# A fused decoder layer whose first projection takes its activations already turned

## The reference

```
def rmsnorm(x, g):
    xf = x.astype(jnp.float32)
    y = xf * lax.rsqrt(jnp.mean(xf * xf, axis=-1, keepdims=True) + EPS)
    return (y * g.astype(jnp.float32)).astype(x.dtype)

def mixer_sublayer(x, k_buf, v_buf, pool_buf, pos0, w_in, w_out, w_pool, pool_scale, sinks, g_pre, g_post):
    h = rmsnorm(x, g_pre)
    proj = jnp.einsum('ntd,de->nte', h, w_in)
    ...                       # q, k, v -> sliding-window attention; u -> causal pooling
    out = jnp.einsum('nte,ed->ntd', jnp.concatenate([a, pl], axis=-1), w_out)
    return x + rmsnorm(out, g_post), new_k, new_v, new_pool

def ffn_sublayer(x, w_up, w_down, g_pre, g_post):
    h = rmsnorm(x, g_pre)
    a = jnp.square(jax.nn.relu(jnp.einsum('ntd,df->ntf', h, w_up)))
    return x + rmsnorm(jnp.einsum('ntf,fd->ntd', a, w_down), g_post)
```

## Time and profile before

| what | value |
|---|---|
| three runs | 2047.56, 2049.05, 2049.23 us, median 2049.05 |
| the profiled execution, its own time | 2047.78 us |
| its span, first to last instruction | 2046.0 us |
| PE busy | 1973.5 us, 96% |
| DVE, ACT, POOL busy | 62%, 60%, 44% |
| mean granted TensorE clock | 0.987 |

### The profile page before, as it was taken

The page is one execution under the profiler, slowest core; times in us unless marked ns, Lnnn a source line. Parts: engine busy times, 40 slices in busy tenths (PEclk is TensorE's granted clock), DMA queues, the critical chain, the costliest instruction groups (busy, mean ns, idle before and its releaser), DMA issues.

```text
span 2046.0 us, 39225 instructions
## 1 busy us (share of the span) xinstructions
PE 1973.5 (96%) x15450; PEld 1941.7 (95%) x15450; DVE 1272.8 (62%) x1966; ACT 1236.2 (60%) x1823; POOL 890.9 (44%) x619
## 2 busy tenths in 40 slices
PE   7999999999988899999999999989999999999998
PEld 6999999899978899999999999989999999999998
DVE  3455543622258776676676676666666666666687
ACT  5234421422264466776776777767777777777784
POOL 0000022211125666766666666654544454444472
PEclk9999998999989899999999999999999999999999
DMA  5411121252233356556556556795656556565542
GB/s 172 165 62 61 55 73 57 77 175 84 92 127 118 122 176 205 170 185 203 174 182 202 177 181 200 228 318 182 213 191 207 181 180 204 185 213 191 182 158 89
DMA packets 271342, 328.16 MB, mean 160 GB/s; under 512 B 8192, under 2 KB 236936, under 8 KB 270063
## 3 DMA queue, kind: packets, MB, share of 16 engines
q1 hardware_dynamic: 267680, 315.66, 47.4%
q10 hardware_dynamic: 3479, 9.99, 1.3%
HBM read 253.79 MB, written 74.22 MB: 160 GB/s over the span
## 4 chain that ended last, share of the span: by engine, by line
PE 59%; DVE 4%; issue 2%; DMA 1%; POOL 1%; ACT 0%; DVEq 0%; SPq 0%; POOLq 0%; ACTq 0%
PE banks L2248 20%; PE banks L2250 19%; PE banks L2249 19%; DVE mlp_rows L1689 3%; DVE quads L1671 1%; DMA mlp_kept<-mlp_rows 1%; DMA mlp_part<-mlp_kept 1%; PE banks L2266 0%; DVE x_tok L1813 0%; ACT mlp_hi L1182 0%; DVE splits L1645 0%; POOL mlp_rows L871 0%; POOL mlp_rows L873 0%; ACT mlp_rows L1176 0%; ACT splits L1159 0%
## 5 line engine op out<-in xcount | busy, mean ns | idle before, releaser
L2248 PE MATMUL banks<-mlp_part,splits 128*128 128x272 f32 x1792 | 517.8, 289 | 6.0 <-DVE y_sum L1668 2.5
L2250 PE MATMUL banks<-mlp_part,splits 128*128 128x272 f32 x1792 | 517.0, 288 | 0.0
L2249 PE MATMUL banks<-mlp_part,splits 128*128 128x272 f32 x1792 | 516.1, 288 | 0.0
L2248 PEld LDWEIGHTS banks<-mlp_part,splits 128*128 128x128 f32 x1792 | 336.6, 188 | 7.4 <-ACT splits L1159 7.0
L2249 PEld LDWEIGHTS banks<-mlp_part,splits 128*128 128x128 f32 x1792 | 340.8, 190 | 0.0
L2250 PEld LDWEIGHTS banks<-mlp_part,splits 128*128 128x128 f32 x1792 | 336.6, 188 | 0.0
L1671 DVE TENSOR_TENSOR y_sum<-y_sum,banks 128x272 f32<-128x272 f32 x416 | 182.2, 438 | 187.7 <-PE banks L2250 187.6
L2248 PE MATMUL banks<-s_part,splits 128*128 128x272 f32 x960 | 279.1, 291 | 7.8 <-ACT splits L1159 3.2
L2250 PE MATMUL banks<-s_part,splits 128*128 128x272 f32 x960 | 278.4, 290 | 0.0
L2249 PE MATMUL banks<-s_part,splits 128*128 128x272 f32 x960 | 277.2, 289 | 0.0
L1857 PE MATMUL banks<-acts_hi,w_hi 128*128 128x272 f32 x1184 | 253.1, 295 | 9.4 <-DVE uT L1357 4.1
(11 more groups left out here) (265 smaller groups left out, 4429.2 us busy)
## 6 DMA issues: line engine op xcount, KB each, us to landing
raw_down<-in_w_down SPq DMA_DIRECT2D x128, 512.0 KB, 4.4
raw_up<-in_w_up SPq DMA_DIRECT2D x120, 512.0 KB, 7.8
mlp_part<-mlp_kept SPq DMA_DIRECT2D x56, 1088.0 KB, 8.3
mlp_kept<-mlp_hi SPq DMA_DIRECT2D x32, 952.0 KB, 4.5
mlp_kept<-mlp_rows SPq DMA_DIRECT2D x32, 952.0 KB, 5.7
w_raw<-in_w_in SPq DMA_DIRECT2D x40, 512.0 KB, 3.5
w_raw<-in_w_out SPq DMA_DIRECT2D x32, 512.0 KB, 3.4
x_kept<-x1T SPq DMA_DIRECT2D x8, 544.0 KB, 2.8
```

Source lines behind the costliest of these rows:

```text
L2248: nc.tensor.matmul(out, wh, xh, start=first, stop=False, skip_group_check=not STARTS[i])
L2249: nc.tensor.matmul(out, wh, xl, start=False, stop=False, skip_group_check=not STARTS[i])
L2250: ins = nc.tensor.matmul(out, wl, xh, start=False, stop=j == pairs - 1, skip_group_check=not STARTS[i])
```

## The change

The host gives x a second time as x_cols, already turned: partition p holds, for each of the 16 tiles, the 544 tokens of feature 128 k + p. It also gives the five norm vectors as one block of columns, vec_cols.

- SP loads vec_cols straight into vecs and x_cols two tiles at a time into x_raw, 8 loads of 557 KB, interleaved with units 0 to 3. x_raw lies where acts_lo lies (tile by tile the same bytes), so the low part of a tile overwrites its raw x.
- No transposes of x, and none of the vectors.
- ACT makes the high part from SBUF, then squares the whole tile into one of two halves of sq_tmp. From the third tile on, the square waits until PE has summed the tile that used this half.
- DVE makes the low part in place, and waits for the high part and for the square.
- PE sums the squares of a tile over partitions with 5 matmuls of one column (`first_sums`, fp32, each two instructions on the engine), issued one tile late, into columns of bank 7. DVE adds the 16 columns per token with two reductions.
- `spread_scales(0)` moves from the end of unit 3 to the middle of unit 4, between its column blocks.
- START_SPLITS, after which tiles the units 1 to 3 are split, goes from 5, 7, 11 to 3, 7, 11.
- POOL's two waits for x and the squares ahead of its masks are gone, as is ACT's issue of four vector loads.

```diff
+        x_raw = at("x_raw", H_AT + KT * T * 4, [P, KT, T])
-        START_SPLITS = {0: 0, 5: 1, 7: 2, 11: 3}
+        START_SPLITS = {0: 0, 3: 1, 7: 2, 11: 3}
...
-            sp.dma_start(pre_rows[:], g_pre_mix[0].rearrange("(k p) -> k p", p=P)).then_inc(vec_landed[0], 16)
+            def load_x(i):
+                sp.dma_start(x_raw[:, 2 * i:2 * i + 2, :], x_cols[:, 2 * i:2 * i + 2, :]).then_inc(x_landed[i], 16)
+
+            sp.dma_start(vecs[:], vec_cols).then_inc(vec_landed[0], 16)
             load_x(0)
...
-                    if pair + kq == 0:
-                        load_x(1)
+                    if pair == 0:
+                        for i in ((1, 2), (3, 4), (5, 6), (7,))[kq]:
+                            load_x(i)
...
-            gp.wait_ge(x_turned, KT)
-            gp.wait_ge(squares, 2 * TOK)
...
             for kt in range(KT):
-                act.wait_ge(x_turned, kt + 1)
-                nc.scalar.activation(acts_hi[:, kt, :], flat(2 * x_slot(kt), T), ACT.Copy, scale=g_pre[:, kt:kt + 1]).then_inc(h_hi, 1)
+                act.wait_ge(x_landed[kt // 2], 16)
+                nc.scalar.activation(acts_hi[:, kt, :], x_raw[:, kt, :], ACT.Copy, scale=g_pre[:, kt:kt + 1]).then_inc(h_hi, 1)
+                if kt >= 2:
+                    act.wait_ge(x_summed, kt - 1)
+                nc.scalar.activation(sq_tmp[:, kt % 2 * T:(kt % 2 + 1) * T], x_raw[:, kt, :], ACT.Square).then_inc(squares, 1)
                 if kt in START_SPLITS:
                     split(START_SPLITS[kt])
-                n = kt - (KT - 2 * TOK)
-                if n >= 0:
-                    half, c = divmod(n, TOK)
-                    r = tok_rows[c]
-                    act.wait_ge(x_landed[half][c], 16)
-                    if n > 0:
-                        act.wait_ge(squares, n)
-                    nc.scalar.activation(uT[0:r].rearrange("p e n -> p (e n)")[:, 0:D // 2],
-                                         x_tok[0:r, c, half * (D // 2):(half + 1) * (D // 2)], ACT.Square,
-                                         accum_out=ss_half[0:r, half, c:c + 1]).then_inc(squares, 1)
             take_root(0)
             split(4)
...
-            dve.wait_ge(pre_ready, 1)
+            dve.wait_ge(vec_landed[0], 16)
             for kt in range(KT):
                 dve.wait_ge(h_hi, kt + 1)
-                nc.vector.scalar_tensor_tensor(out=acts_lo[:, kt, :], in0=flat(2 * x_slot(kt), T), scalar=g_pre[:, kt:kt + 1],
+                dve.wait_ge(squares, kt + 1)
+                nc.vector.scalar_tensor_tensor(out=acts_lo[:, kt, :], in0=x_raw[:, kt, :], scalar=g_pre[:, kt:kt + 1],
                                                in1=acts_hi[:, kt, :].bitcast(F32), op0=ALU.mult, op1=ALU.subtract).then_inc(h_lo, 1)
                 if kt in START_SPLITS:
                     split(START_SPLITS[kt])
-            dve.wait_ge(squares, 2 * TOK)
-            step(nc.vector.tensor_tensor(ss[:], ss_half[:, 0, :], ss_half[:, 1, :], ALU.add))
+            dve.wait_ge(consts, 3)
+            dve.wait_ge(x_summed, KT)
+            by_tile = banks[:, 7, P:P + TOK * KT].rearrange("p (c k) -> p c k", k=KT)
+            nc.vector.tensor_reduce(ss[:, 0:TOK - 1], by_tile[:, 0:TOK - 1, :], AX.X, ALU.add)
+            step(nc.vector.tensor_reduce(ss[0:ND, TOK - 1:TOK], by_tile[0:ND, TOK - 1:TOK, :], AX.X, ALU.add))
...
+            def first_sums(kt):
+                pe.wait_ge(squares, kt + 1)
+                for c in range(TOK):
+                    rows = tok_rows[c]
+                    at = kt % 2 * T + c * P
+                    ins = nc.tensor.matmul(banks[0:rows, 7, P + c * KT + kt:P + c * KT + kt + 1], sq_tmp[:, at:at + rows],
+                                           ones[:, 0:1], start=True, stop=True)
+                ins.then_inc(x_summed, 1)
+
+            def first_tiles(q):
+                for kk in range(UNIT_KT):
+                    kt = q * UNIT_KT + kk
+                    pe.wait_ge(h_lo, kt + 1)
+                    for nt in range(2):
+                        ins = product(slot(nt), q % SPLIT_SLOTS, kk, nt, acts_hi[:, kt, :], acts_lo[:, kt, :], kt == 0, kt == KT - 1)
+                        if nt == 0 and kt == KT - 1:
+                            ins.then_inc(first_done, 1)
+                    if kk == UNIT_KT - 1:
+                        ins.then_inc(unit_used, 1)
+                    if kt > 0:
+                        first_sums(kt - 1)
+                    if kt == KT - 1:
+                        first_sums(kt)
...
-                if j == K_UNITS - 1:
-                    spread_scales(0)
...
                     if j == K_UNITS and nt == 1:
+                        spread_scales(0)
                         pe.wait_ge(scale_ready, 1)
```

More of the change, by code:

```diff
@@ L264, in hybrid_decoder @@
         dec_probs = sq_tmp[:, 0:4 * NKEY].rearrange("p (c k) -> p c k", c=4)
-        vec_landed = [sem(f"vec_landed{i}") for i in range(7)]
-        x_landed = [[sem(f"x_landed{i}_{c}") for c in range(TOK)] for i in range(2)]
+        vec_landed = [sem(f"vec_landed{i}") for i in range(3)]
+        x_landed = [sem(f"x_landed{i}") for i in range(KT // 2)]
         x2_landed = [sem(f"x2_landed{i}") for i in range(TOK)]
@@ L283, in hybrid_decoder @@
         vecs_ready = sem("vecs_ready")
-        pre_turned = sem("pre_turned")
-        pre_ready = sem("pre_ready")
         small = sem("small")
         squares = sem("squares")
+        x_summed = sem("x_summed")
         x_turned = sem("x_turned")
@@ L385, in dec_out @@
             return src, qT[r, 0:QT, SEQ:T].rearrange("d (pair e) (b t) -> d e pair b t", pair=PAIRS, t=DEC_T)[:, e]
-        def x_slot(kt):
-            return kt if kt < 2 else 2 + kt % 2
-        START_SPLITS = {0: 0, 5: 1, 7: 2, 11: 3}
+        START_SPLITS = {0: 0, 3: 1, 7: 2, 11: 3}
         Y_RING = 7
@@ L650, in _ @@
             store_x1(7)
-            sp.wait_ge(x_turned, 2 * KT)
+            sp.wait_ge(x_turned, KT)
             load_late(2)
@@ L939, in _ @@
             take_root(0)
             split(4)
-            act.wait_ge(x_turned, KT)
-            act.wait_ge(squares, 2 * TOK)
+            act.wait_ge(squares, KT)
             act.dma_start(state_tok, state_pool[0].rearrange("b s c -> (b s) c")).then_inc(state_landed, 16)
-            rows = [(g_post_mix, 0, KT), (g_pre_ffn, KT, KT), (g_post_ffn, 2 * KT, KT), (pool_scale, 3 * KT, UT)]
-            for i, (vec, at, n) in enumerate(rows):
-                act.dma_start(vec_rows[at:at + n, :], vec[0].rearrange("(k p) -> k p", p=P)).then_inc(vec_landed[i + 1], 16)
@@ L1881, in pair_tiles @@
                         between(q, 1)
-            def tile_by_tile(u, pair, rows, q, half_way):
+            def first_sums(kt):
[6 more added lines that the diff above has]
+                ins.then_inc(x_summed, 1)
@@ L1885, in tile_by_tile @@
+            def first_tiles(q):
                 for kk in range(UNIT_KT):
                     kt = q * UNIT_KT + kk
-                    pe.wait_ge(h_lo, rows + kt + 1)
+                    pe.wait_ge(h_lo, kt + 1)
                     for nt in range(2):
-                        if kt == 0 and nt == 1:
-                            pe.wait_ge(h_lo, rows + 2)
-                        if kt == 0 and pair >= 2:
-                            pe.wait_ge(tile_read, 2 * pair - 3 + nt)
-                        ins = product(slot((pair % 2) * 2 + nt), u % SPLIT_SLOTS, kk, nt, acts_hi[:, kt, :],
-                                      acts_lo[:, kt, :], kt == 0, kt == KT - 1)
+                        ins = product(slot(nt), q % SPLIT_SLOTS, kk, nt, acts_hi[:, kt, :], acts_lo[:, kt, :], kt == 0, kt == KT - 1)
@@ L1915, in _ @@
-            for kt in range(UNIT_KT):
-                first_turn(kt)
+                    if kk == UNIT_KT - 1:
[4 more added lines that the diff above has]
+                        first_sums(kt)
+            pe.wait_ge(consts, 6 + 2 * GQA + PAIRS)
             def turn_new_keys():
@@ L1941, in turn_vectors @@
                 pe.wait_ge(consts, 7 + 2 * GQA + PAIRS)
-                for i in range(1, 7):
+                for i in range(1, 3):
                     pe.wait_ge(vec_landed[i], 16)
                 pe.wait_ge(old_k_act, 2)
-                n = 3 * KT + UT
-                nc.tensor.transpose(banks[:, 4, 0:n], vec_rows, ident[0:n, 0:n])
                 nc.tensor.matmul(banks[:, 5, 0:HEADS], ones[0:1, 0:1].broadcast_to([1, P]), sink_row, start=True, stop=True)
@@ L2109, in _ @@
                 if pair == 0:
-                    tile_by_tile(j, 0, 0, q, mid)
-                    after(j)
+                    first_tiles(q)
                     continue
@@ L2303 @@
     depth, dec_b, window, kv_heads, hd = inputs['cache_k'].shape
+    d = inputs['x_prompt'].shape[-1]
+    x = np.concatenate([inputs['x_prompt'].reshape(-1, d), inputs['x_sample'].reshape(-1, d)])
+    x_cols = np.ascontiguousarray(x.T.reshape(d // P, P, -1).transpose(1, 0, 2))
```

(5 more changed lines are left out.)

48 lines of the change are left out of this document (7 added, 41 removed).

## The result

| | before | after |
|---|---|---|
| median of four runs on one chip | 2049.1 us (2047.56 to 2049.23) | 2110.72 us (2109.08 to 2112.53) |
| ratio, 95% interval | | 1.030 (1.0284 to 1.0317) |
| profiled execution, its span | 2047.78, 2046.0 us | 2109.92, 2108.2 us |
| mean granted clock | 0.987 | 0.965 |
| first product, start of unit 5 | 17.31, 61.75 us | 10.29, 122.85 us |

The change makes the kernel 3.0% slower, 62 us. That is outside my range of 2079 to 2104, and 19 us above the forecast of 2092. Nearly all of it lies before unit 5, which starts 61.1 us later; what follows takes 1985.35 us in place of 1984.25. Of the executions of all kernels here one is left out of its ratio: one of the seven of experiment 9 took 4984.95 us, the other six 2041.88 to 2044.01, and nothing on record says why.

A forecast was written before the change was run, and what follows sets the result against it. PE's own instructions were taken to bound the kernel. Unit 5 starting 31.8 us late, 3 for clock falls at the pair's end and 9 in the loop made 43.8 on 2047.8: 2091.6, given as 2092; range 2079 to 2104.

The forecast's parts named there:

- The chain: Loop, tiles 2 to 15: square, low part and products cannot overlap the previous tile's products; 4.33 us per tile, 60.6 in all.
- The start: Before the first product: loads, high part, split and low part let it begin at 10.3 us, 7.0 earlier.
- the first sums: After the first two tiles' products, partly at the low clock: PE begins summing squares at 14.6 us.
- the low part at 0.78: DVE in the loop: the low part, both inputs from SBUF, takes 0.78 us while POOL is idle.
- the clock: In the loop: six falls to the low clock at 1.5 us each, 9 us; bounds 0 and 17 to 27.
- rival 2: In the loop: the clock stays low throughout, 17 to 27 us in place of 9; 2100 to 2110 us; chance 0.08.
- Rival 1: In the loop: the clock holds; 2082.6 us, or 2079.6 if the end's gaps cost nothing; chance 0.17.
- The end of the pair: From last sums to unit 5: gaps of 3.5 and 4.2 us, 77.4 to 93.5; their clock falls add 3.0.
- The early load of the root's function table: ACT, end of the pair: the 1.28 us load is hidden by the last products; otherwise it adds 1.3.
- The sums: PE, per tile: one-column sums take 1.20 us until another engine continues, 0.97 for PE; PE's work 2.48 against 2.29.
- rival 4: In the loop: the wait hides, PE bound by its own instructions at 2.7 us per tile; 2057 us; chance 0.03.
- rival 5: In the loop: sums cost nothing and the wait hides, 1.51 us per tile; faster, 2039 us; chance 0.04.

The follow-up runs named there:

- experiment 9: Changed kernel with POOL adding the squares, PE summing once, and the splits of units 4 and 5 earlier in their queues: 2043.34 us, ratio 0.9971.
- experiment 1: Changed kernel with 12 unread matmuls of 272 columns behind each tile's sums, filling PE's wait: 2084.62 us, ratio 1.0174.
- (2): Changed kernel with a ring of three buffers for the squares instead of two halves, sums still one tile late: 2058.71 us, ratio 1.0049.
- (3): Changed kernel with each tile's sums issued right behind its own products, two halves kept: 2065.5 us, ratio 1.0081.
- (5): Changed kernel with raw x in a place of its own, so the low part waits for no square: 2066.75 us, ratio 1.0088.
- experiment 6: Changed kernel with the spread of the scales back at the end of unit 3: 2101.1 us, ratio 1.0257.
- experiment 7: Changed kernel with unit 4's splits ahead of root and reductions, DVE's unit 5 split ahead of reading the keys: 2102.1 us, ratio 1.0258.
- experiment 8: Changed kernel with three buffers for the squares and the splits of units 4 and 5 earlier in their queues: 2051.03 us, ratio 1.001.
- experiment 10: Changed kernel with float32r squares as moving operand against one ones column, accumulated in PSUM; three square buffers, splits earlier: 2038.71 us, ratio 0.9947.
- experiment 4: Changed kernel with sums right behind their own tile's products, plus 24 identity transposes on PE before the first product: 2064.12 us, ratio 1.0069.

## Why the prediction was wrong

**The chain was right.** The period at the full clock is 4.34 (experiment 1) for 4.33. Cutting it at two places, the buffer (2) and the order (3), removes all of PE's waits in the loop, and cutting the link from the square to the low part (5) all but three. The start, 10.29 for 10.3, the first sums at 15.22 for 14.6, and the low part at 0.78 beside an idle POOL came as worked out.

**The term that failed is the clock**, "I take six falls at 1.5: 9". The last sums end at 104.4 us where the sum without the clock has 77.4: of the 27.0, 0.6 come from the start and 26.4 from the loop, 17.4 more than I took. Experiment 1 gives 26.1 for the same. With 26.4 in place of 9 the sum is 61.2, against 61.1 at unit 5 and 62.1 in the profiled execution. A tile at the low clock takes 6.41 for 4.33, 2.08 more, just above my 1.2 to 1.9, so 26.4 is the price of nearly 13 tiles of 14. The size is not fixed: the same loop lost 3.9 less in the profiled execution of experiment 6. The reason that fell is "while the products are dense enough to bring it back". The earlier trace rows showed one rise, behind products without a pause, and the 15 slow matmuls behind the gap of the earlier trace rows ended in another of that kind; from them I took that a tile's products would bring one every two or three turns. The trace after shows three stretches of 27 us each, the last of them reaching past the loop, in which they don't. In rival 2 I had the price right, 17 to 27, and gave it 0.08. I had no row that told of a rise with one-column matmuls and idle time in each turn. With none, the upper bound deserved as much weight as the middle; my range left most of it out. The Trainium skill, "TensorE: Matmul & The Clock Gate", section "A second HAM failure mode: psum-queue depth-cycling", says that short idle stretches between groups of matmuls, if they come often enough, let the clock swing back and forth; the trace after agrees, with 14 gaps of 1.63 to 1.73 and a few short rises. I had not weighed it, and it speaks for rival 2. Rival 1, the clock that holds, is experiment 1: 2084.6 for 2082.6.

**The end of the pair** was right within a microsecond: from the last sums to unit 5 18.45 us, and 1.1 more behind it, for 16.1 + 3. The clock did not come as told, though: it had been low since 86 us, so that the first of the two gaps brought no fall, and only the second did, behind unit 5. The two stalls with their clock are worth 8.6 in the medians of experiment 7, part of which is the loop's, and 7.7 in those of experiment 8, for 3.5 + 4.2 + 3 = 10.7. The early load of the root's function table was hidden, as said.

**The sums** were 1.20 for PE in my sum, and 1.13 from the end of the products to the start of the square at the high clock (15.22 to 16.35). That PE's work per tile grows even without the chain, 2.48 for 2.29, fits in kind; the runs show 2.64, as the first pair of matmuls behind the sums starts 1.03 after their start, not 0.97, and the next pair 0.36 after that, not 0.25. So rival 4 with 2.7 per tile, 2057, is what the ring of three measured, 2058.7; rival 5 needed below 2.1 per tile, and 1.75 gave 2038.7 (experiment 10) for its 2039. That these two agree is in part luck: experiment 10 has the splits moved as well, and rival 5 had not.

## What to carry to other kernels

A ring of two gives no overlap when its slot is given back one tile late: count, for each buffer, behind whose products the release stands, and ask which engine's next step waits for the writer. Short waits that recur in every turn of a loop must be priced at both clock levels for the whole loop, and not per fall; a single rise seen beside dense work says nothing of work with gaps. Ahead of making an engine's queue longer, look at what is queued behind a waiting instruction: here the order of a few lines was worth 8 us, and which operand of the sums is loaded as weights (128 columns or one), with the rounding that went with it, 0.9 us per tile. And a difference of a few us between kernels with such a loop is not all that of the edit: the same loop, untouched, differed by 3.9 us from one profiled execution to another.

## What the runs showed of the hardware

- PE busy for 10.00 of 10 us can have the low clock: in experiment 3 four tiles with one-column sums between the products took 4.7 us each, until 32 us. The clock column reads 1.00 in that stretch all the same, and 0.50 for the same pace in experiment 4, so a 1.00 at the start of a trace can't be trusted. In experiment 5 both stand together: 0.50 from about 36 to 43 us, with PE busy throughout. The pace of matmuls of one shape tells the level: 0.25 per pair of 272 columns at 2.4 GHz, 0.45 at 1.2.
- What raised the clock and what kept it differ. Products with sums between kept it to the end of the pair (experiments 2 and 4), but had not raised it more than 20 us after the first product in experiment 3, and had after 9 in experiment 4. What makes this difference is open.
- A one-column matmul in fp32 with 128x128 of weights costs PE 0.11 us for each of its two instructions at the high clock, the same sum with the operands exchanged and rounded to float32r 0.125 for 272 columns.
- In experiment 9 an addition of 128x544 on POOL takes 1.78 us, and DVE's two-input instructions beside it take up to twice their time (on average 1.60 for 0.78, and 2.11 for 1.23).
